# Inverting in halves of four matrices, and other shares of gathered rows for each layer, in a two-block transformer kernel

## Chip, cores and metric

The kernel runs on one core of one Trainium2 chip. The metric is the device time of one execution in microseconds. Three runs of the kernel before gave 3375.44 us in the median (3370.27 to 3380.55).

## The reference, cut to what matters

Two blocks work on 256 tokens of 1024 features in float32. The first block has two layers. In each, `h = rms_norm(x)`, one projection gives the inputs of three mixers (rwkv7, dilated attention, latent attention), their results go through `w_out`, and a gated feed-forward follows. The second block has two layers with attention and a PEER layer, for 256 latent tokens, and in its first layer also for 256 context tokens. The PEER layer picks 128 experts per token (8 heads, the best 16 each):

```python
u = u_tab[expert]                              # rows of 1024 numbers, one per slot
act = gelu(einsum('nhkd,nd->nhk', u, h))
out = einsum('nhk,nhkd->nd', g * act, v_tab[expert])
```

The rwkv7 scan is `state = state * w - (state kk) b + v k` over 256 steps. The kernel computes it in chunks of 64 steps, which needs the inverses of eight 128 x 128 unit triangular matrices (four heads, two tiles of 128 tokens; the two chunks of a tile lie on the matrix's diagonal).

## The kernel before, in words

**Stages.** The program is a row of stages. Each has its own code for each engine, and at its end TensorE (PE), ScalarE (ACT), VectorE (DVE) and SyncE (SP) join. First come the context tokens' own stages, then for each layer l = 0, 1 of the first block `in_projection`, `rwkv`, `latent_heads`, `first_attention`, `out_projection`, `feed_forward`, then the second block. GpSimd (POOL) doesn't join: it runs through one list of gathers on its own.

**Context rows.** The context tokens' PEER layer is independent of the first block, so its rows are spread over the first block's stages. There are 2 x 2 x 128 = 512 of them: for each half (blk) of the context tokens 128 rows of `u` (v = 0 in `order`) and 128 rows of `v` (v = 1). One row is a gather of 128 experts x 1024 float32, 0.524 MB, by `fetch` on POOL (L1318), and one instruction of 128x1024 on DVE: the dot product of a u row (L1338) or the weighted sum of a v row (L1335). `take(v, n, name)` (L1324 on) puts n of them into the code of a stage, `take_rest` the remainder of the stage's share. The shares are `SHARE` for either layer and `TAIL_SHARE` for the first attention of the second block. The u rows of half l must all lie ahead of layer l's feed-forward, where `weigh` makes the weights out of the dot products. `CTX_TAIL = 24` v rows of each half go to the end of the list.

**Places.** A row lands in one of four places of `ctx_ring`, or of four more in `ctx_more`. rwkv uses `ctx_more` for its matrices, so its rows have the four narrow places only (`wide` returns -1); in the other stages of the first block there are eight. POOL gathers a row into a place when DVE has used the place's last row (`ctx_used`).

**Weights.** SP loads groups of weights (2.1 MB for 4096 numbers per partition, in four pieces of 512 KB) into a ring of three slots. It loads group n + 3 when PE has finished group n.

**The inversion in rwkv (L579 to L771).** `b.inv` and `b.invT` hold eight matrices and their transposes. DVE masks the triangle (`keep(1, ...)`, L749), and for each of six levels selects the level's part into `b.ms` (L756). PE multiplies `ms` by `inv` (L586, 8 products, `w_done`), ACT copies the result to `b.ws` (L695), PE makes the updates of both (L597, L598, 16 products, `upd_done`), and DVE subtracts them from `inv` and `invT` in two instructions of 128x1024 (L770). Between these, PE does one half each of a group of modulation products (L1518, `mod_part`), and DVE takes six rows per level. Each float32 product is two passes in the trace. On DVE the order in a level is: wait for `w_done` of the level before, select, six rows, wait for `upd_done`, two subtractions. Everything works on all eight matrices at once.

**After it.** Four chunks with 2, 4, 4 and 4 rows, then the output (L793) with takes of 4, 2 and 3 rows as far as the share goes (4 and 1 here, L797 and L802 follow), and the group norm.

**Feed-forward.** PE computes 22 tiles of gate and up products (L1187), each of 32 products with a 128x256 result, into four buffers. Tile j waits for `acted` of tile j - 4. DVE multiplies gate and up (L1225, L1226) and then takes its rows: 2 or 3 by turns in layer 0, which also carries routing steps, 4 in layer 1. The down projection (L1199) follows, 352 passes, tile by tile in order of `acted`. DVE adds the result (L1244) when it is done.

## Time and profile before

| | us |
|---|---|
| median of 3 runs | 3375.44 |
| profiled execution, its time | 3365.98 |
| its span | 3364.1 |
| PE busy | 2677.2 (80%) |
| DVE busy | 2247.5 (67%) |
| POOL busy | 1211.3 (36%) |
| ACT busy | 586.3 (17%) |

The DMA engines moved 1029.23 MB, 306 GB/s in the mean. The chain that ended last is 39% PE, 30% DMA and 22% DVE. By place in the span: the context stages lie before 283 us, layer 0 of the first block from 283 to 926, layer 1 from 926 to 1548, and the second block behind that; its two PEER layers make the last 1500 us, with the DMA engines at 420 GB/s. Busy times are sums over stages with different limits, so they must be read stage by stage. Stage borders are read from the timelines.

### The profile page before, as it was taken

The numbers are of one execution on the slowest core, as the hardware profiler recorded it, in microseconds if no ns is written. First come the engines' busy times: TensorE is split into PE (matmuls) and PEld (weight loads), VectorE is DVE, ScalarE is ACT, GpSimd is POOL, SyncE is SP. The second block draws the span as 40 slices with busy tenths as digits, with TensorE's granted clock in tenths as the row PEclk, the third lists the DMA queues.
The fourth block names the chain that finished last, engine by engine and source line by source line (L and its number), as shares of the span: only waits on it lengthen the run. The fifth ranks groups of instructions, "written<-read, shape, count | busy, mean of one in ns | idle before, by whom it ended". The sixth has DMA issues, their size and how long they took to land.

```text
span 3364.1 us, 30927 instructions
## 1 busy us (share of the span) xinstructions
PE 2677.2 (80%) x10160; PEld 1779.6 (53%) x10160; DVE 2247.5 (67%) x5413; ACT 586.3 (17%) x1601; POOL 1211.3 (36%) x1028
## 2 busy tenths in 40 slices
PE   6898676899685869998887877777789977777776
PEld 2787555688574747886575332322247833323222
DVE  0538876788768576774958985655555499856555
ACT  1311201200011021001311111111124111111111
POOL 0002443345644424651323444444300044444442
PEclk8998776999897678998999999999989989999999
DMA  9337785789977657995657999999930379999997
GB/s 394 113 133 257 274 293 202 242 312 343 392 292 276 220 196 253 409 409 195 202 183 296 402 420 420 420 420 420 410 122 31 138 323 419 420 420 420 420 418 307
DMA packets 209376, 1029.23 MB, mean 306 GB/s; under 512 B 23392, under 2 KB 24928, under 8 KB 142784
## 3 DMA queue, kind: packets, MB, share of 16 engines
q0 software_dynamic: 147456, 805.37, 61.1%
q1 hardware_dynamic: 60480, 215.77, 17.1%
q10 hardware_dynamic: 1280, 6.11, 0.5%
q8 instruction: 81, 1.33, 0.2%
q14 instruction: 79, 0.65, 0.1%
HBM read 1021.98 MB, written 5.18 MB: 305 GB/s over the span
## 4 chain that ended last, share of the span: by engine, by line
PE 39%; DMA 30%; DVE 22%; issue 5%; ACT 2%; POOL 1%; SPq 1%; DVEq 0%; ACTq 0%; another core or an unknown queue 0%; POOLq 0%
DMA w_ring<-in_peer_uv,expert 16%; PE ps L1187 9%; PE ps L2251 4%; PE ps L1940 4%; DMA ctx_ring<-in_peer_uv,expert 4%; DMA own<-in_peer_uv,expert 4%; PE ps L1109 4%; PE ps L443 4%; PE ps L1648 3%; PE ps L1199 2%; DVE ctx_ring L1338 2%; DMA ctx_ring<-in_peer_u,ctx_expert 2%; DVE sum L1335 2%; DVE w_ring L2128 2%; DMA w_ring<-in_weights 2%
## 5 line engine op out<-in xcount | busy, mean ns | idle before, releaser
L2251 PE MATMUL ps<-w_ring,diag 128*128 128x512 f32 x1224 | 586.9, 620 | 177.4 <-ACT diag L2210 177.4
L2128 DVE SCALAR_TENSOR_TENSOR w_ring<-w_ring,htok 128x1024 f32<-128x1024 f32 x306 | 374.4, 1224 | 216.5 <-DMA w_ring<-in_peer_uv,expert 214.6
L2251 PEld LDWEIGHTS ps<-w_ring,diag 128*128 128x128 f32 x1224 | 228.7, 196 | 527.3 <-ACT diag L2210 286.6
L2098 POOL DMA_INDIRECT w_ring<-in_peer_uv,expert x306 | 337.5, 1103 | 447.7 <-PE ps L2251 396.7
L1318 POOL DMA_INDIRECT ctx_ring<-in_peer_u,ctx_expert x192 | 247.5, 1289 | 579.9 <-DVE ctx_ring L1338 299.1
L1187 PE MATMUL ps<-mix,w_ring 128*128 128x256 f32 x1408 | 309.3, 383 | 7.4 <-DVE mix L388 7.4
L1187 PEld LDWEIGHTS ps<-mix,w_ring 128*128 128x128 f32 x1408 | 270.8, 193 | 45.9 <-issue 8.2
L2210 ACT ACTIVATE diag<-consts_sb,w 128x128 f32<-128x128 f32 x512 | 177.6, 394 | 604.0 <-DVE w L2145 600.0
L1318 POOL DMA_INDIRECT ctx_ring<-in_peer_v,ctx_expert x148 | 184.0, 1243 | 235.4 <-DVE sum L1335 159.9
L2251 PE MATMUL ps<-ctx_ring,diag 128*128 128x512 f32 x416 | 212.0, 637 | 67.7 <-ACT diag L2210 67.7
L1338 DVE SCALAR_TENSOR_TENSOR ctx_ring<-ctx_ring,h_now 128x1024 f32<-128x1024 f32 x192 | 228.3, 1223 | 54.1 <-DMA ctx_ring<-in_peer_u,ctx_expert 46.2
L2098 POOL DMA_INDIRECT own<-in_peer_uv,expert x52 | 53.7, 1033 | 412.2 <-DVEq L1875 296.5
L1318 POOL DMA_INDIRECT ctx_more<-in_peer_v,ctx_expert x108 | 136.4, 1263 | 140.3 <-DVE low L1335 59.7
L2251 PEld LDWEIGHTS ps<-ctx_ring,diag 128*128 128x128 f32 x416 | 78.8, 199 | 190.1 <-ACT diag L2210 108.5
L2128 DVE SCALAR_TENSOR_TENSOR ctx_ring<-ctx_ring,htok 128x1024 f32<-128x1024 f32 x104 | 127.2, 1223 | 70.6 <-DMA ctx_ring<-in_peer_uv,expert 70.2
L2251 PE MATMUL ps<-own,diag 128*128 128x512 f32 x208 | 108.3, 645 | 81.3 <-ACT diag L2210 81.3
L2098 POOL DMA_INDIRECT ctx_ring<-in_peer_uv,expert x104 | 115.9, 1115 | 150.4 <-PE ps L2251 147.4
L1199 PE MATMUL ps<-act,w_ring 128*128 128x256 f32 x704 | 152.3, 379 | 0.0
L1199 PEld LDWEIGHTS ps<-act,w_ring 128*128 128x128 f32 x704 | 133.8, 190 | 18.2
L1940 PE MATMUL ps<-hT,w_ring 128*128 128x256 f32 x512 | 120.3, 391 | 13.3 <-DVE hT L385 13.3
L2205 ACT ACTIVATE th<-th 128x2 f32<-128x2 f32 x256 | 52.0, 203 | 450.2 <-DVE th L2137 450.2
L443 PE MATMUL ps<-mix,w_ring 128*128 128x256 f32 x544 | 119.7, 382 | 6.1 <-DVE mix L388 6.1
(402 smaller groups left out, 4553.9 us busy)
## 6 DMA issues: line engine op xcount, KB each, us to landing
w_ring<-in_weights SPq DMA_DIRECT2D x392, 512.0 KB, 8.0
w_ring<-in_peer_uv,expert POOLq DMA_INDIRECT x306, 15.9
ctx_ring<-in_peer_u,ctx_expert POOLq DMA_INDIRECT x192, 5.6
ctx_ring<-in_peer_v,ctx_expert POOLq DMA_INDIRECT x148, 8.8
consts_sb<-in_consts ACTq DMA_DIRECT2D x1, 1867.0 KB, 9.8
ctx_more<-in_peer_v,ctx_expert POOLq DMA_INDIRECT x108, 10.8
ctx_ring<-in_peer_uv,expert POOLq DMA_INDIRECT x104, 15.9
cT_first<-in_ctx_by_feature ACTq DMA_DIRECT2D x1, 1024.0 KB, 15.8
```

The source lines that it names most:

```text
L443: ins = pe.matmul(m.ps[:, j % BANKS, 0:SEQ], w[:, k, c:c + P], m.hT[:, k, 0:SEQ], start=(k == 0), stop=(k == KT - 1))
L1109: ins = pe.matmul(m.ps[:, j, 0:SEQ], w[:, k, (j % 4) * P:(j % 4 + 1) * P], src[:, k, 0:SEQ], start=(k == 0), stop=(k == KT - 1))
L1187: ins = pe.matmul(m.ps[:, GU[j % 4], part * SEQ:(part + 1) * SEQ], w[:, k, (j % 2) * P:(j % 2 + 1) * P], m.hT[:, k, 0:SEQ], start=(k == 0) ...
L1199: ins = pe.matmul(m.ps[:, 2 + o // 2, (o % 2) * SEQ:(o % 2 + 1) * SEQ], w[:, kk, o * P:(o + 1) * P], b.act[:, j, :], start=(j == 0 and o % ...
L1318: pool.indirect_dma_start(out=self.slot(r), out_offset=None, in_=expert_tables(self.d)[v], in_offset=bass.IndirectOffsetOnAxis(ap=m.ctx_ex ...
L1338: v.scalar_tensor_tensor(out=row, in0=row, scalar=1.0, in1=m.h_now[:, :], op0=ALU.mult, op1=ALU.mult, accum_out=m.ctx_dots[:, k:k + 1]).th ...
L1648: ins = pe.matmul(m.ps[:, j % 4, 0:width(j)], w[:, k, (j % 4) * P:(j % 4 + 1) * P], m.hT[:, k, 0:width(j)], start=(k == 0), stop=(k == KT ...
L1940: ins = pe.matmul(m.ps[:, j % 4, 0:SEQ], w[:, k, (j % 4) * P:(j % 4 + 1) * P], m.hT[:, k, 0:SEQ], start=(k == 0), stop=(k == KT - 1))
L2098: pool.indirect_dma_start(out=entry(e), out_offset=None, in_=table, in_offset=bass.IndirectOffsetOnAxis(ap=m.expert[:, blk, k:k + 1], axis ...
L2128: v.scalar_tensor_tensor(out=u, in0=u, scalar=1.0, in1=m.htok[:, blk, :], op0=ALU.mult, op1=ALU.mult, accum_out=b.dots[:, e:e + 1]).then_i ...
L2210: act.activation(b.diag[:, e % DIAGS, :], m.ident, ACT.Copy, scale=b.w[:, e:e + 1]).then_inc(s.built, 1)
L2251: ins = pe.matmul(m.ps[:, 2 * blk + half, :], b.diag[:, e % DIAGS, :], entry(e)[:, D + half * 512:D + (half + 1) * 512], start=(k == 0), s ...
```

## The change

It has two parts. (1) The inversion works in halves h of four matrices: PE, ACT and DVE signal each half on its own, the subtractions become four instructions of 128x512, `inv` and `invT` get a semaphore each, the next level is selected ahead of the subtractions, four rows are taken per level and none in level 0. (2) The shares are different for each layer; `CTX_TAILS` leaves 40 v rows of the first half and 24 of the second for later. Layer 1's feed-forward takes all 104 of its own half and the first 16 of the first half's 40.

| share | in_projection | rwkv | latent_heads | attention | out_projection | feed_forward |
|---|---|---|---|---|---|---|
| before, both layers | 28 | 64 | 8 | 16 | 12 | 104 |
| after, layer 0 | 36 | 56 | 8 | 16 | 12 | 88 |
| after, layer 1 | 36 | 56 | 8 | 16 | 12 | 120 |

The tail goes from 14, 18, 16 (project_qkv, attention, out_projection) to 16, 18, 14. `wide` is as before.

```diff
-CTX_TAIL = 24
+CTX_TAILS = (40, 24)
...
-                rows.take(v, 3, "in_projection")
+                rows.take(v, 4, "in_projection")
...
+        four = lambda i, h: m.ps[:, i + h, :].rearrange("p (c t) -> p c t", c=4)
...
                 pe.wait_ge(s.level_ready, lev + 1)
-                if lev:
-                    pe.wait_ge(s.upd_copied, 2 * lev)
-                for i in range(8):
-                    x = m.ident if lev == 0 else b.inv[:, i, :]
-                    ins = pe.matmul(m.ps[:, i // 4, (i % 4) * P:(i % 4 + 1) * P], b.ms[:, i, :], x,
-                                    start=True, stop=True)
-                ins.then_inc(s.w_done, 1)
+                for h in range(2):
+                    if lev:
+                        pe.wait_ge(s.inv_copied, 2 * (lev - 1) + h + 1)
+                    for i in range(4 * h, 4 * h + 4):
+                        x = m.ident if lev == 0 else b.inv[:, i, :]
+                        ins = pe.matmul(m.ps[:, h, (i % 4) * P:(i % 4 + 1) * P], b.ms[:, i, :], x, start=True, stop=True)
+                    ins.then_inc(s.w_done, 1)
...
                 mod_part(lev, 0, 1)
-                pe.wait_ge(s.w_copied, lev)
-                for i in range(8):
-                    xt = b.invT[:, i, :]
-                    pe.matmul(m.ps[:, 2 + i // 4, (i % 4) * P:(i % 4 + 1) * P], xt, b.ws[:, i, :], start=True, stop=True)
-                    ins = pe.matmul(m.ps[:, 4 + i // 4, (i % 4) * P:(i % 4 + 1) * P], b.ws[:, i, :], xt,
-                                    start=True, stop=True)
-                ins.then_inc(s.upd_done, 1)
+                for h in range(2):
+                    pe.wait_ge(s.w_copied, 2 * (lev - 1) + h + 1)
+                    pe.wait_ge(s.invT_copied, 2 * (lev - 1) + h + 1)
+                    for i in range(4 * h, 4 * h + 4):
+                        xt = b.invT[:, i, :]
+                        pe.matmul(m.ps[:, 2 + h, (i % 4) * P:(i % 4 + 1) * P], xt, b.ws[:, i, :], start=True, stop=True)
+                        ins = pe.matmul(m.ps[:, 4 + h, (i % 4) * P:(i % 4 + 1) * P], b.ws[:, i, :], xt, start=True, stop=True)
+                    ins.then_inc(s.upd_done, 1)
                 mod_part(lev, 1, 2)
...
-                act.wait_ge(s.w_done, lev + 1)
-                act.activation(b.ws[:, :, :], two_banks(0), ACT.Copy).then_inc(s.w_copied, 1)
+                for h in range(2):
+                    act.wait_ge(s.w_done, 2 * lev + h + 1)
+                    act.activation(b.ws[:, 4 * h:4 * h + 4, :], four(0, h), ACT.Copy).then_inc(s.w_copied, 1)
...
+            keep(1, b.mt, "before", 0)
+            select_level(0)
+            for h in range(2):
+                link(v.tensor_tensor(quad(b.invT, h), eye, quad(b.ms, h), ALU.subtract), s.invT_copied)
+            for h in range(2):
+                v.wait_ge(s.w_done, h + 1)
+                link(v.tensor_tensor(quad(b.inv, h), eye, four(0, h), ALU.subtract), s.inv_copied)
+            select_level(1)
+            keep(2, b.mkt, "before", 6)
+            for lev in range(1, LEVELS):
+                rows.take(v, 4, "rwkv")
+                if lev + 1 < LEVELS:
+                    v.wait_ge(s.w_done, 2 * lev + 2)
+                    select_level(lev + 1)
+                for dst, bk, copied in ((b.inv, 2, s.inv_copied), (b.invT, 4, s.invT_copied)):
+                    for h in range(2):
+                        v.wait_ge(s.upd_done, 2 * (lev - 1) + h + 1)
+                        link(v.tensor_tensor(quad(dst, h), quad(dst, h), four(bk, h), ALU.subtract), copied)
...
-                    rows.take(v, 4, "feed_forward")
+                    rows.take(v, 5, "feed_forward")
...
-        kept = SLOTS - CTX_TAIL
+        kept = [SLOTS - tail for tail in CTX_TAILS]
```

`select_level` is the selection of L756, and `quad(dst, h)` is half h of the eight matrices.

## Rows read from the trace of the kernel before

**Rows 1.** Windows: PE, PEld, DVE, ACT, POOL busy, PEclk, DMA share, GB/s.

```profile
283.00:363.50 80.50, 73.87 (x320) 63.64 (x320) 60.54 (x150) 13.20 (x32) 33.45 (x28) 0.94 0.78 281
399.60:480.50 80.90, 55.10 (x336) 41.27 (x336) 62.39 (x84) 8.11 (x10) 40.00 (x33) 0.77 0.81 284
894.00:926.00 32.00, 0.00 (x0) 0.00 (x0) 21.20 (x22) 0.04 (x1) 16.74 (x16) 0.54 1.03 409
1312.00:1469.60 157.60, 154.64 (x705) 135.78 (x706) 114.64 (x126) 11.21 (x25) 89.05 (x73) 0.98 0.96 378
1380.00:1410.00 30.00, 30.00 (x141) 26.41 (x140) 21.39 (x23) 1.82 (x5) 18.16 (x16) 1.00 1.03 409
```

**Rows 2.** DVE timeline, layer 0's inversion (start, us, line, [idle before]).

```profile
419.44 2.47 DVE L770 TENSOR_TENSOR ctx_more<-ctx_more,ps 128x1024 f32<-128x1024 f32 x2
...
435.65 2.47 DVE L770 TENSOR_TENSOR ctx_more<-ctx_more,ps 128x1024 f32<-128x1024 f32 x2
438.16 1.23 DVE L756 TENSOR_TENSOR ms<-ctx_more,consts_sb 128x1024 f32<-128x1024 f32 x1
439.42 1.23 DVE L1338 SCALAR_TENSOR_TENSOR ctx_ring<-ctx_ring,h_now 128x1024 f32<-128x1024 f32 x1
...
440.57 1.22 DVE L1338 SCALAR_TENSOR_TENSOR ctx_ring<-ctx_ring,h_now 128x1024 f32<-128x1024 f32 x1
...
477.95 2.47 DVE L770 TENSOR_TENSOR ctx_more<-ctx_more,ps 128x1024 f32<-128x1024 f32 x2
```

**Rows 3.** timeline of PE in the same inversion, level 2.

```profile
423.22 3.79 PE L586 MATMUL ps<-ctx_more,ms 128*128 128x128 f32 x16 [3.11 <-DVE ms L756]
426.94 1.94 PE L1518 MATMUL ps<-w_ring,silu 128*32 128x512 f32 x8
...
432.73 1.06 PE L1518 MATMUL ps<-w_ring,silu 128*32 128x512 f32 x8
```

**Rows 4.** chain of waits in the same inversion (start, us, what).

```profile
426.69 7.79 DMA ctx_ring<-in_peer_u,ctx_expert
...
471.59 5.19 DMA ctx_ring<-in_peer_u,ctx_expert
```

**Rows 5.** timeline of DVE, a 128x512 instruction that reads PSUM.

```profile
398.86 0.69 DVE L745 TENSOR_TENSOR rk<-ps,low 128x512 f32<-128x512 f32 x1
```

**Rows 6.** timeline of DVE at the end of layer 0's rwkv.

```profile
539.76 0.69 DVE L797 SCALAR_TENSOR_TENSOR yc<-ps,cum 128x512 f32<-128x512 f32 x1 [0.55 <-PE ps L653]
...
544.14 3.35 DVE L802 RECIPROCAL sq<-sq 128x512 f32<-128x512 f32 x1 [2.96 <-ACT sq L701]
```

**Rows 7.** timeline of DVE, end of layer 0's in_projection, start of rwkv.

```profile
354.07 1.23 DVE L1338 SCALAR_TENSOR_TENSOR ctx_more<-ctx_more,h_now 128x1024 f32<-128x1024 f32 x1 [1.54 <-DMA ctx_more<-in_peer_u,ctx_expert]
...
363.53 0.74 DVE L707 TENSOR_SCALAR kk<-low,vectors 128x256 f32<-128x256 f32 x2 [0.55 <-DVE ctx_weight L1893]
```

**Rows 8.** timeline of DVE at the end of layer 0's feed-forward.

```profile
883.21 1.28 DVE L1335 SCALAR_TENSOR_TENSOR sum<-ctx_ring,ctx_weight,sum 128x1024 f32<-128x1024 f32 x1 [1.22 <-DMA ctx_ring<-in_peer_v,ctx_expert]
...
923.23 2.48 DVE L1244 TENSOR_TENSOR xT<-xT,ps 128x512 f32<-128x512 f32 x4
```

**Rows 9.** timeline of PE in layer 0's feed-forward.

```profile
817.68 76.14 PE L1199 MATMUL ps<-act,w_ring 128*128 128x256 f32 x352
```

**Rows 10.** timeline of DVE, start of layer 1's rwkv.

```profile
1003.45 0.74 DVE L707 TENSOR_SCALAR kk<-low,vectors 128x256 f32<-128x256 f32 x2 [18.49 <-SPq L169]
```

**Rows 11.** timeline of DVE in layer 1's feed-forward.

```profile
1356.71 1.28 DVE L1335 SCALAR_TENSOR_TENSOR low<-ctx_more,ctx_weight,low 128x1024 f32<-128x1024 f32 x1 [0.56 <-DMA ctx_more<-in_peer_v,ctx_expert]
...
1489.60 0.41 DVE L1225 TENSOR_TENSOR act<-sg,ps 128x256 f32<-128x256 f32 x1
...
1545.66 2.48 DVE L1244 TENSOR_TENSOR xT<-xT,ps 128x512 f32<-128x512 f32 x4 [11.86 <-PE ps L1199]
```

**Rows 12.** timeline of DVE, end of the second block's first out_projection.

```profile
1720.62 0.48 DVE L1133 SCALAR_TENSOR_TENSOR xT<-ps,mods,xT 128x256 f32<-128x256 f32 x1
...
1727.86 1.75 DVE L379 RECIPROCAL htok<-htok 128x256 f32<-128x256 f32 x1 [0.34 <-DVEq L169]
```

More of the change, by code:

```diff
@@ L495, in rwkv @@
     sems = ("step_v step_a step_p acted lora_done ready_kk kk_sum kk_root ready_bonus bonus_sum bonus_used scaled turned tok_done "
-            "pairs_done masked level_ready w_done w_copied upd_done upd_copied rhs_done rhs_copied sa_done sa_copied "
+            "pairs_done masked level_ready w_done w_copied upd_done inv_copied invT_copied rhs_done rhs_copied sa_done sa_copied "
             "grow_done state_ready y_done y_copied mean_done centered var_done var_root act_tanh mod_done mod_copied mod_kept0 mod_kept1")
@@ L593, in _ @@
                 mod_part(lev, 0, 1)
-                pe.wait_ge(s.w_copied, lev)
-                for i in range(8):
-                    xt = b.invT[:, i, :]
-                    pe.matmul(m.ps[:, 2 + i // 4, (i % 4) * P:(i % 4 + 1) * P], xt, b.ws[:, i, :], start=True, stop=True)
-                    ins = pe.matmul(m.ps[:, 4 + i // 4, (i % 4) * P:(i % 4 + 1) * P], b.ws[:, i, :], xt,
-                                    start=True, stop=True)
-                ins.then_inc(s.upd_done, 1)
+                for h in range(2):
[6 more added lines that the diff above has]
+                    ins.then_inc(s.upd_done, 1)
                 mod_part(lev, 1, 2)
-            pe.wait_ge(s.upd_copied, 2 * LEVELS)
+            pe.wait_ge(s.inv_copied, 2 * LEVELS)
+            pe.wait_ge(s.invT_copied, 2 * LEVELS)
             pe.wait_ge(s.masked, 2)
@@ L750, in keep, with select_level @@
                                      ALU.mult), s.masked)
-            keep(1, b.mt, "before", 0)
-            for lev in range(LEVELS):
-                if lev:
-                    v.wait_ge(s.w_done, lev)
+            def select_level(lev):
                 link(v.tensor_tensor(b.ms[:, :, :], b.mt[:, :, :],
@@ L758, in _ @@
                      s.level_ready)
-                if lev == 0:
-                    keep(2, b.mkt, "before", 6)
-                rows.take(v, 6 if lev else 2, "rwkv")
-                if lev == 0:
-                    v.wait_ge(s.w_done, 1)
-                    eye = m.ident.unsqueeze(1).broadcast_to([P, 8, P])
-                    link(v.tensor_tensor(b.inv[:, :, :], eye, two_banks(0), ALU.subtract), s.upd_copied)
-                    link(v.tensor_tensor(b.invT[:, :, :], eye, b.ms[:, :, :], ALU.subtract), s.upd_copied)
-                    continue
-                v.wait_ge(s.upd_done, lev)
-                for dst, bk in ((b.inv, 2), (b.invT, 4)):
-                    link(v.tensor_tensor(dst[:, :, :], dst[:, :, :], two_banks(bk), ALU.subtract), s.upd_copied)
+            eye = m.ident.unsqueeze(1).broadcast_to([P, 4, P])
+            quad = lambda dst, h: dst[:, 4 * h:4 * h + 4, :]
+            keep(1, b.mt, "before", 0)
[16 more added lines that the diff above has]
+                        link(v.tensor_tensor(quad(dst, h), quad(dst, h), four(bk, h), ALU.subtract), copied)
             v.sem_inc(s.state_ready, 1)
@@ L1252 @@
 class ContextRows:
-    SHARE = dict(in_projection=28, rwkv=64, latent_heads=8, attention=16, out_projection=12, feed_forward=104)
-    TAIL_SHARE = dict(project_qkv=14, attention=18, out_projection=16)
+    FIRST_SHARE = dict(in_projection=36, rwkv=56, latent_heads=8, attention=16, out_projection=12, feed_forward=88)
+    SECOND_SHARE = dict(in_projection=36, rwkv=56, latent_heads=8, attention=16, out_projection=12, feed_forward=120)
+    TAIL_SHARE = dict(project_qkv=16, attention=18, out_projection=14)
     def __init__(self, m, d):
         self.m, self.d = m, d
-        kept = SLOTS - CTX_TAIL
-        self.order = [(blk, v, k) for blk in range(TT) for v, n in ((0, SLOTS), (1, kept)) for k in range(n)]
-        self.order += [(blk, 1, k) for blk in range(TT) for k in range(kept, SLOTS)]
+        kept = [SLOTS - tail for tail in CTX_TAILS]
+        self.order = [(blk, v, k) for blk in range(TT) for v, n in ((0, SLOTS), (1, kept[blk])) for k in range(n)]
+        self.order += [(blk, 1, k) for blk in range(TT) for k in range(kept[blk], SLOTS)]
         self.taken = 0
         self.ends, at, stage_of = {}, 0, []
-        for l, share in enumerate((self.SHARE, self.SHARE, self.TAIL_SHARE)):
+        for l, share in enumerate((self.FIRST_SHARE, self.SECOND_SHARE, self.TAIL_SHARE)):
             for name, n in share.items():
```

## The prediction

> **What bounds the kernel now.** I read the stages one by one in the windows, then the timelines of DVE and PE across each edit, the chain of waits inside the inversion, and at each stage's end the wait that was last. The second block's two PEER layers make the last 1500 us and aren't touched; all that counts lies between 283 and 1728 us.
>
> In the inversion DVE is on the path, and in it the rows. From one pair of subtractions to the next DVE needs (477.95 - 419.44) / 4 = 14.6 us [rows 2]. Of this 2.5 us are the two subtractions, 1.26 the selection (438.16 to 439.42), and the rest, over 10 us, six rows: four lie ready in the ring and cost 1.15 us each (439.42 to 440.57, rows 2), the last two wait for their gathers, which take 5.19 to 7.79 us from issue to landing [rows 4]. PE is done earlier. In level 2 it multiplies for 3.79 us, works 1.94 us on the modulation, about 3.9 us on the updates (to 432.73) and 1.06 us on the modulation again [rows 3], 10.5 us together, but DVE's subtraction comes 2.8 us after the updates, which ended at 432.7 (435.65, rows 2).
>
> Layer 0's in_projection ends with DVE's rows and the softmax of the routing at 363.5 [rows 7]. Its feed-forward ends with DVE too: PE's last product ends at 817.68 + 76.14 = 893.8 [rows 9], the addition starts at 923.23 [rows 8], and PE stands still between them, while the DMA engines are full at 409 GB/s [rows 1]. Layer 1's in_projection leaves DVE 18.5 us idle at its end [rows 10]. Layer 1's feed-forward ends with PE, DVE waits 11.86 us for it [rows 11]. So rows were too many in layer 0's feed-forward and there is room in layer 1, but how much room is the question of the sum.
>
> **Inversion (both layers).** Per level DVE has four rows (4 x 1.15 = 4.6), a selection (1.26) and four subtractions of 128x512. The nearest row, an instruction of that size on PSUM, takes 0.69 us and the next starts 0.72 later [rows 5]; with the wait on its own semaphore 0.73, so 2.92. Sum 8.8 us, if nothing stalls. PE's order lets it multiply the first half as soon as that half of `inv` is subtracted, while DVE does the other three, so its 10.5 us are the other bound; they hold both clock levels: 16 passes take 3.79 us after the 3.11 us wait, 0.23 each (1.2 GHz), while the updates' 32 passes take 3.9 us [rows 3], 0.12 each (2.4 GHz). With shorter waits the first part should run at the upper level more often (1.9 and 1.1 us), which gives 7.8. The ring is the third: a gather that starts 1.5 us after the first row and is landed 5.2 to 7.8 us later; the fourth is issued 6.0 us after the first row, so its place is ready at 11.2 to 13.8 and is wanted at 8.8 + 3.5 = 12.3. With the short landing nothing waits, with the long one 1.5 us. I take 9.6 us, halfway between 8.8 and 10.5: four intervals give 38.4 for 58.5, that is -20. The start (no rows in level 0, halves instead of the second wait for PE) lets the first subtraction begin at about 416 instead of 419.44 [rows 2], -3; the last four halves take 0.4 more than two wholes. Sum -23 per layer; bounds -26 (8.8) and -16 (10.5 everywhere and the start worth nothing).
>
> **End of rwkv.** The takes of 2 and 3 were cut to 1 and 0 by the share; now they are whole. Before L797 DVE waited 0.55 us after one row [rows 6]: a second row adds 0.6. Before L802 it waited 2.96 us: three rows take 3.45, and the third lies in a place freed only four microseconds earlier, so 1.5 more. Together +2.1 per layer (bounds 1 and 4). rwkv is thus -20.9 in each layer, -41.8 in both.
>
> **in_projection.** Eight more rows in each layer, 9.2 us of DVE. In layer 0 DVE is busy throughout, the last rows wait already (1.54 us, rows 7), and after them, from 356.6 to 362.4, it waits for ACT's softmax: 9.2 + 2 - 6 = +5 (bounds 3 and 9). In layer 1 they lie under the 18.5 us [rows 10]; but the stage now starts without the 32 us of full-rate transfers, and 0.5 to 4 us may come late: +1 (0 to 6).
>
> **Feed-forward of layer 0.** 16 fewer rows, all from its end, where they came one per 1.9 us (21 rows from 883.21 to 922.4, rows 8). DVE would be through at about 891, so PE's 893.8 ends the stage: 923.23 - 894.0 = -29.2. If the 13 last rows come later than now, DVE ends it: bound -25.
>
> **Feed-forward of layer 1.** This is where it is paid. The DMA engines are full there: 1380 to 1410 at 409 GB/s [rows 1]. A tile needs four rows (2.10 MB) and half a group of weights (1.05 MB). PE takes 7.03 us per tile (154.64 us for 22, rows 1) and so its weights take 149 GB/s, which leaves 260 for rows: one per 2.02 us. The trace agrees: from the first late row (the 19th, 1356.71) to tile 21's multiplication behind row 84 (1489.60) it is 132.9 us for 66 rows, 2.01 each [rows 11]. Five rows per tile then take 10.1 us, more than PE's 7.03, and PE may be only four tiles ahead. Tile j's products start at about 1315 + 7.03 j; the multiplication of tile j - 4 stands behind row 5 (j - 4), at 1277.4 + 10.1 j in this count. They meet at j = 12, and from 13 on PE waits. Both then share the DMA engines: (5 x 0.524 + 1.05) / 0.409 = 9.0 us per tile. Tile 21 starts at 1277.4 + 131.3 + 8 x 9.0 = 1480.7 instead of 1462.6: +18 at the down projection, which follows in 76.1 us, and so at the stage's end. The 11.86 us of DVE's slack don't help, since the delay arises ahead of the down projection. Bounds: +9, if only the end counts (16 rows at 1.28 us, full rate, less the slack), and +32, 16 rows at 2.02.
>
> The Trainium skill ("DMA: Bandwidth & Descriptors", section "Where 436 GB/s comes from") says that a transfer between HBM and SBUF is bound by the HBM side at about 358 GB/s per core. By that rule a tile would take 10.2 us and this term would be about +28. The trace disagrees, it holds 409 GB/s for 30 us at a time; the sum goes by the trace.
>
> **Tail.** project_qkv gets two rows more on a DVE that is the bound there, 2 x 1.25 = +2.5. out_projection gets two less: its last addition starts at 1720.62 and the next stage at 1727.86 [rows 12], where the same step without rows takes about 3 us. -4.2 (0 to -5).
>
> **Sum.** -41.8 + 5 + 1 - 29.2 + 18 + 2.5 - 4.2 = -48.7 us. The profiled execution, 3365.98 (span 3364.1), becomes 3317.3. It stands 9.5 below the median of the runs, so for the median 3375.4 - 48.7 = 3326.7, and 3327 is the forecast. The large uncertain terms are the level (2 x 5), layer 1's feed-forward (9 to 14) and the base (5). In quadrature that is about 17: 3312 to 3342 as the forecast's own range.
>
> **Rivals.**
> (a) *The rows in layer 1's feed-forward cost their full 2.02 us*, because PE's wait delays weights in turn: +32 instead of +18, 3341. For it: the DMA engines are at 1.03 there, nothing gives way. Against it: PE's wait itself lowers the weights' rate.
> (b) *They cost only what passes the end*: +9, and the inversion reaches 8.8: 3375.4 - 48.7 - 9 - 6 = 3312, with layer 0's in_projection at its lower bound 3310. For it: PE's buffers and the ring's prefetch, which I count coarsely. Against it: row 84's time, which fits the 2.02 to 1%.
> (c) *TensorE stays at 1.2 GHz in the whole inversion*, since its bursts get shorter and waits more frequent. 48 passes at 0.23 and 2 x 1.94 are 14.9 us per level, as long as now: the inversion gains nothing, 3375.4 - 48.7 + 46 = 3373, no change. For it: 3.79 us after each wait and a mean clock of 0.77 there [rows 1]. Against it: the updates are at full clock in each level already, and the waits shrink. The Trainium skill ("TensorE: Matmul & The Clock Gate", section "HAM oscillation — how this bites in real kernels") describes bursts of products between waits that start slow every single time; the first part of rows 3 agrees.
> (d) *Slower: the DMA engines bind the whole first block.* What leaves layer 0's feed-forward is 8.4 MB moved at 409 GB/s while PE stood still; if in_projection of layer 1 then waits for those bytes, 20.5 us are given back, the eight rows of each in_projection cost 8 x 2.02 = 16.2, layer 1's feed-forward +32, and the inversion stays at 10.5 (-16 + 2.1 per layer). Sum: 16.2 + 16.2 + 20.5 + 32 - 27.8 - 29.2 - 1.7 = +26, 3401. It decides if the share of in_projection, 0.78 in layer 0 [rows 1], comes to 1 with 4.2 MB more: 22.6 MB in 80.5 us become 26.8, 333 GB/s, below 409. That speaks against it.
> That the change doesn't do what it says isn't a case: the shares are read at build time and sum to 512, and `wide` is as before.
>
> **How the numbers follow.** Forecast 0.60, (a) 0.17, (b) 0.13, (c) 0.06, (d) 0.04. The range that holds 8 in 10 reaches to (b) with its spread below and past (a) above: 3303 to 3352. A measurement of this kernel tells 0.3%, 10 us, from none (its three runs span 0.3%). Faster by more than that: all of the forecast, (a) and (b), less a little, plus a part of (c): 0.90. Within it: 0.06. Slower: 0.04.
>
> **What would show it.** Inversion: starts of the selection (L756's successor) 9 to 10 us apart, and no row waiting over 1.5 us; at 14 or more (c) is right. PE's first part of a level at 1.9 us instead of 3.79. Layer 0's feed-forward: the addition within 1 us behind PE's last product, DVE waiting for PE. Layer 1: steps of 9 us per tile in the second half, tile products that wait for DVE's `act` (in sum about 18 us), a down projection without gaps, DVE done before it. Layer 0's in_projection: rwkv 3 to 9 us later from its start. The forecast is wrong if layer 1's in_projection ends with rows, if the down projection waits for weights, or if either inversion takes over 65 us between its first mask and the first chunk (81 now).

## The result, and the profile after

The kernel after takes 3333.15 us in the median of 4 runs (3328.32 to 3340.96), the kernel before in the same comparison 3376.32. The ratio is 0.9876, with a 95% interval of 0.9848 to 0.9903. The forecast was 3327. The profiled execution took 3328.75 (span 3326.9, before 3364.1), so the two traces differ by 37.2 us where the forecast's sum had 48.7. The differences by stage follow (two figures are layer 0 / layer 1; the marks are rounded, so the rows add to 37.5):

| stretch | before | after | difference | forecast |
|---|---|---|---|---|
| layer 0 in_projection | 80.4 | 86.0 | +5.6 | +5 |
| rwkv up to the first mask | 36.1 / 36.3 | 35.5 / 39.2 | +2.3 | 0 |
| first mask to last subtraction, layer 0 / 1 | 80.8 / 81.0 | 58.3 / 60.3 | -43.2 | -46 |
| chunks, to the copies of y | 55.7 / 63.1 | 63.2 / 57.1 | +1.5 | 0 |
| end of rwkv | 14.4 / 13.9 | 16.1 / 15.7 | +3.5 | +4.2 |
| latent heads to out_projection | 110.3 / 114.9 | 113.0 / 114.8 | +2.6 | 0 |
| layer 0 feed-forward | 262.4 | 233.0 | -29.4 | -29.2 |
| layer 1 in_projection | 77.4 | 77.3 | -0.1 | +1 |
| layer 1 feed-forward | 233.1 | 255.1 | +22.0 | +18 |
| second block's first attention stages | 182.2 | 180.0 | -2.2 | -1.7 |
| all else | | | -0.1 | 0 |

From its first mask to the first subtraction layer 0 now takes 420.18 - 406.34 = 13.8 us (19.9 before). The level in the inversion, DVE's timeline of layer 0, answers to [rows 2]. L780 is now four subtractions merged to one line, L757 the selection, L1349 a row:

```profile
420.18 2.85 DVE L780 TENSOR_TENSOR ctx_more<-ctx_more,ps 128x512 f32<-128x512 f32 x4
423.07 1.23 DVE L1349 SCALAR_TENSOR_TENSOR ctx_ring<-ctx_ring,h_now 128x1024 f32<-128x1024 f32 x1
...
428.78 1.23 DVE L1349 SCALAR_TENSOR_TENSOR ctx_ring<-ctx_ring,h_now 128x1024 f32<-128x1024 f32 x1 [3.33 <-DMA ctx_ring<-in_peer_u,ctx_expert]
...
431.33 1.23 DVE L1349 SCALAR_TENSOR_TENSOR ctx_ring<-ctx_ring,h_now 128x1024 f32<-128x1024 f32 x1 [1.32 <-DMA ctx_ring<-in_peer_u,ctx_expert]
...
432.48 1.22 DVE L757 TENSOR_TENSOR ms<-ctx_more,consts_sb 128x1024 f32<-128x1024 f32 x1
433.74 2.85 DVE L780 TENSOR_TENSOR ctx_more<-ctx_more,ps 128x512 f32<-128x512 f32 x4
...
441.87 1.23 DVE L1349 SCALAR_TENSOR_TENSOR ctx_ring<-ctx_ring,h_now 128x1024 f32<-128x1024 f32 x1 [1.65 <-DMA ctx_ring<-in_peer_u,ctx_expert]
...
444.28 2.85 DVE L780 TENSOR_TENSOR ctx_more<-ctx_more,ps 128x512 f32<-128x512 f32 x4
```

The four subtractions take 2.85 us. The steps are 13.6 and 10.5, then 9.0 and 8.5 (the next two starts are 453.29 and 461.83): the two long ones hold rows that wait for their gathers, 3.33 + 1.32 us in the first and 1.65 in the second. The same levels on PE, in answer to [rows 3] (L588 the products of `ms` and `inv`):

```profile
421.01 2.02 PE L588 MATMUL ps<-ctx_more,ms 128*128 128x128 f32 x16
422.96 1.06 PE L1529 MATMUL ps<-w_ring,silu 128*32 128x512 f32 x8
...
434.57 3.75 PE L588 MATMUL ps<-ctx_more,ms 128*128 128x128 f32 x16 [5.77 <-DVE ctx_more L780]
```

In this layer they ran at 1.2 GHz once (3.75 us), behind a wait of 5.77 us, and at 2.4 GHz in the other levels (2.02 to 2.05).

The ends of layer 0's in_projection (DVE; [rows 7]) and feed-forward (PE, then DVE; [rows 8, 9]):

```profile
362.24 1.23 DVE L1349 SCALAR_TENSOR_TENSOR ctx_more<-ctx_more,h_now 128x1024 f32<-128x1024 f32 x1 [4.28 <-DMA ctx_more<-in_peer_u,ctx_expert]
...
370.79 0.35 DVE L711 TENSOR_SCALAR kk<-low,vectors 128x256 f32<-128x256 f32 x1 [0.55 <-DVE ctx_weight L1904]
```

```profile
849.81 40.09 PE L1209 MATMUL ps<-act,w_ring 128*128 128x256 f32 x185
```

```profile
890.01 2.48 DVE L1254 TENSOR_TENSOR xT<-xT,ps 128x512 f32<-128x512 f32 x4 [1.38 <-PE ps L1209]
```

Layer 0's in_projection ends with rows, one of them 4.28 us late. Layer 1's ends with a row as well: PE is done at 967.3, the last row waits 1.32 us for its gather and starts at 968.57, and rwkv starts at 970.15. In rwkv three more rows wait, 3.2 us in all:

```profile
968.57 1.23 DVE L1349 SCALAR_TENSOR_TENSOR ctx_more<-ctx_more,h_now 128x1024 f32<-128x1024 f32 x1 [1.32 <-DMA ctx_more<-in_peer_u,ctx_expert]
...
973.70 1.23 DVE L1349 SCALAR_TENSOR_TENSOR ctx_ring<-ctx_ring,h_now 128x1024 f32<-128x1024 f32 x1 [0.54 <-DMA ctx_ring<-in_peer_u,ctx_expert]
...
976.28 1.23 DVE L1349 SCALAR_TENSOR_TENSOR ctx_ring<-ctx_ring,h_now 128x1024 f32<-128x1024 f32 x1 [1.34 <-DMA ctx_ring<-in_peer_u,ctx_expert]
...
978.84 1.23 DVE L1349 SCALAR_TENSOR_TENSOR ctx_ring<-ctx_ring,h_now 128x1024 f32<-128x1024 f32 x1 [1.33 <-DMA ctx_ring<-in_peer_u,ctx_expert]
```

The feed-forward of layer 0 ends with PE, and DVE waits for it. Layer 1's feed-forward on PE, where [rows 11] showed DVE waiting only at the end:

```profile
1259.81 85.63 PE L1197 MATMUL ps<-mix,w_ring 128*128 128x256 f32 x384 [3.71 <-DVE mix L388]
1347.47 7.14 PE L1197 MATMUL ps<-mix,w_ring 128*128 128x256 f32 x32 [2.02 <-DVE act L1236]
1356.49 8.86 PE L1197 MATMUL ps<-mix,w_ring 128*128 128x256 f32 x32 [1.88 <-DVE act L1236]
...
1419.68 16.84 PE L1197 MATMUL ps<-mix,w_ring 128*128 128x256 f32 x64 [3.23 <-DVE act L1236]
1436.36 76.14 PE L1209 MATMUL ps<-act,w_ring 128*128 128x256 f32 x352
```

384 records are 12 tiles; from the thirteenth on (j = 12) PE waits for `act`, and ten tiles take 1436.36 - 1347.47 = 88.9 us, 8.9 each in the mean (9.0 forecast, 7.03 without waits). Windows of the two kernels, first before (chunks of layer 0 and 1, feed-forward of layer 1), then after; the columns are those of [rows 1], so the third figure from the end is the granted clock, the mean of a stretch (0.5 is 1.2 GHz throughout, 1.0 is 2.4):

```profile
480.40:536.10 55.70, 46.99 (x304) 45.20 (x304) 29.69 (x55) 2.82 (x5) 24.81 (x18) 0.75 0.63 217
1120.70:1183.80 63.10, 54.35 (x304) 52.54 (x304) 29.70 (x56) 2.82 (x5) 24.80 (x18) 0.65 0.57 197
1312.50:1545.70 233.20, 230.67 (x1056) 202.36 (x1056) 156.67 (x164) 11.32 (x25) 121.51 (x100) 0.99 0.97 378
```

```profile
406.30:464.70 58.40, 42.98 (x336) 32.65 (x336) 49.81 (x73) 8.96 (x15) 26.04 (x21) 0.94 0.79 285
464.70:527.90 63.20, 54.46 (x304) 52.65 (x304) 29.71 (x55) 2.81 (x5) 24.75 (x18) 0.65 0.58 197
1069.70:1126.90 57.20, 48.42 (x304) 46.61 (x304) 29.72 (x56) 2.82 (x5) 24.75 (x18) 0.73 0.65 219
1257.40:1512.50 255.10, 239.10 (x1056) 205.96 (x1056) 176.62 (x179) 11.29 (x25) 145.23 (x116) 0.96 0.96 378
```

The inversion now runs at a mean clock of 0.94. The chunks, which the change doesn't touch, do the same 304 products in 55.7 to 63.2 us, and the clock goes with the length in both kernels: PE's idle time in a chunk phase (length less PE busy) is 8.7 to 8.8 us in all four. In the feed-forward PE is busy 8.4 us longer with the same products (a part of them at 1.2 GHz) and idle 13.5 us longer: 22.

### The profile page after: what moved, and what is told of

Same layout as the page of the kernel before. It is cut to its first block, busy times and chain, and to the rows that moved or that the text cites. A ratio compares the mean times of both kernels' runs of the same rounds, so it can differ in the third digit from the quotient of the medians.

```text
span 3326.9 us, 31010 instructions
## 1 busy us (share of the span) xinstructions
PE 2671.1 (80%) x10160; PEld 1773.6 (53%) x10160; DVE 2249.5 (68%) x5437; ACT 587.6 (18%) x1611; POOL 1216.9 (37%) x1028
## 3 DMA queue, kind: packets, MB, share of 16 engines
q0 software_dynamic: 147456, 805.37, 61.7%
## 4 chain that ended last, share of the span: by engine, by line
PE 35%; DMA 34%; DVE 21%; issue 5%; POOL 3%; ACT 1%; SPq 1%; DVEq 0%; ACTq 0%; POOLq 0%
DMA w_ring<-in_peer_uv,expert 16%; PE ps L1197 5%; PE ps L2262 5%; PE ps L1209 5%; PE ps L1951 4%; DMA own<-in_peer_uv,expert 4%; DMA ctx_ring<-in_peer_uv,expert 4%; PE ps L1119 4%; DMA ctx_ring<-in_peer_u,ctx_expert 3%; PE ps L1659 3%; DMA ctx_ring<-in_peer_v,ctx_expert 2%; DVE ctx_ring L1349 2%; DMA w_ring<-in_weights 2%; POOL ctx_ring L1329 2%; DVE w_ring L2139 1%
## 5 line engine op out<-in xcount | busy, mean ns | idle before, releaser
L2262 PE MATMUL ps<-w_ring,diag 128*128 128x512 f32 x1224 | 595.6, 629 | 171.7 <-ACT diag L2221 171.4
L1329 POOL DMA_INDIRECT ctx_ring<-in_peer_u,ctx_expert x184 | 237.1, 1288 | 558.8 <-DVE ctx_ring L1349 270.1
L1197 PE MATMUL ps<-mix,w_ring 128*128 128x256 f32 x1408 | 317.7, 389 | 21.0 <-DVE act L1236 13.6
L1349 DVE SCALAR_TENSOR_TENSOR ctx_ring<-ctx_ring,h_now 128x1024 f32<-128x1024 f32 x184 | 218.2, 1223 | 36.4 <-DMA ctx_ring<-in_peer_u,ctx_expert 28.5
L2262 PE MATMUL ps<-own,diag 128*128 128x512 f32 x208 | 107.1, 639 | 80.4 <-ACT diag L2221 80.4
L1329 POOL DMA_INDIRECT ctx_more<-in_peer_u,ctx_expert x72 | 89.2, 1240 | 113.8 <-DVE ctx_more L1349 52.2
## 6 DMA issues: line engine op xcount, KB each, us to landing
w_ring<-in_peer_uv,expert POOLq DMA_INDIRECT x306, 15.9
ctx_more<-in_peer_v,ctx_expert POOLq DMA_INDIRECT x108, 10.3
ctx_ring<-in_peer_uv,expert POOLq DMA_INDIRECT x104, 15.9
```

The costliest lines, as they stand in the source:

```text
L1197: ins = pe.matmul(m.ps[:, GU[j % 4], part * SEQ:(part + 1) * SEQ], w[:, k, (j % 2) * P:(j % 2 + 1) * P], m.hT[:, k, 0:SEQ], start=(k == 0) ...
L1329: pool.indirect_dma_start(out=self.slot(r), out_offset=None, in_=expert_tables(self.d)[v], in_offset=bass.IndirectOffsetOnAxis(ap=m.ctx_ex ...
L1349: v.scalar_tensor_tensor(out=row, in0=row, scalar=1.0, in1=m.h_now[:, :], op0=ALU.mult, op1=ALU.mult, accum_out=m.ctx_dots[:, k:k + 1]).th ...
L2262: ins = pe.matmul(m.ps[:, 2 * blk + half, :], b.diag[:, e % DIAGS, :], entry(e)[:, D + half * 512:D + (half + 1) * 512], start=(k == 0), s ...
```

## The experiments

Each is compared with runs of the kernel before on the same chip, whose median was between 3369 and 3377 us in the different comparisons. So kernels of different comparisons are told apart by their ratios and by the traces' stretches, not by a few microseconds between medians. All are edits of the kernel after, unless said. The tables give the same stretches as above, layer 0 / layer 1.

**1. Halves and rows apart.** First part (1) of the change without its fewer rows, called halves here: the split, the two semaphores, and the selection ahead of the subtractions.

```diff
-CTX_TAILS = (40, 24)                                  +CTX_TAILS = (24, 24)
-shares of the change                                  +28, 64, 8, 16, 12, 104 in both layers
-rows.take(v, 4, "rwkv")        # each level           +rows.take(v, 6, "rwkv")
```

> The inversion in halves, but the shares of before everywhere (28, 64, 104 in both layers, six rows in each level). My theory (the rows held the level, the halves only let PE overlap the subtractions): DVE still needs 6 x 1.15 + 1.26 + 2.9 = 11.1 us per level and two of its rows wait for their gathers, so 13 to 14 us per level instead of 14.6; first mask to last subtraction 76 to 80 us (before 80.8), about 3 to 5 us per layer, 3366 to 3372 in all. Rival (the halves alone make the gain): levels of 10.4 us as in the changed kernel, 60 us, 3336.

Shares only:

```diff
-for h in range(2): ...                     # PE, ACT, DVE by halves
+ins = pe.matmul(...) for all eight, one w_done, upd_done, upd_copied as before
+if lev: rows.take(v, 4, "rwkv")
```

> The new shares with the old inversion (all eight matrices at once), four rows per level and none in level 0. My theory: the level is now PE's chain, 2.5 of subtractions, 2 to 3.8 of the first products, 1.9 of the modulation and 3.9 of the updates, 10.5 to 12 us; inversion 62 to 68 us instead of 58.3 with the halves, so 3341 to 3352. Rival 1 (halves are worth nothing, only the rows counted): 58 us, 3333 as the changed kernel. Rival 2 (the halves were nearly all): 14 us per level, 78 us, 3372.

| | time, ratio (95%) | inversion | in_projection 0 | feed-forward |
|---|---|---|---|---|
| before | 3376.9 | 80.8 / 81.0 | 80.4 | 262.4 / 233.1 |
| halves only | 3372.1, 0.9987 (0.9973 to 1.0) | 81.6 / 79.9 | 77.9 | 262.6 / 233.1 |
| shares only | 3353.1, 0.9919 (0.9894 to 0.9945) | 69.4 / 71.2 | 87.6 | 233.2 / 255.9 |
| after | 3333.2, 0.9876 | 58.3 / 60.3 | 86.0 | 233.0 / 255.1 |

Halves alone are worth nothing that the runs can tell (I had expected inversions of 76 to 80 us), four rows alone 10 to 11 us per layer, both together 21 to 23. DVE's timeline with halves and six rows, then with four rows and no halves (L772 and L757 are its subtractions and selection):

```profile
434.81 2.85 DVE L780 TENSOR_TENSOR ctx_more<-ctx_more,ps 128x512 f32<-128x512 f32 x4
...
449.24 2.85 DVE L780 TENSOR_TENSOR ctx_more<-ctx_more,ps 128x512 f32<-128x512 f32 x4
```

```profile
438.63 2.48 DVE L772 TENSOR_TENSOR ctx_more<-ctx_more,ps 128x1024 f32<-128x1024 f32 x2 [5.07 <-PE ps L599]
441.14 1.23 DVE L757 TENSOR_TENSOR ms<-ctx_more,consts_sb 128x1024 f32<-128x1024 f32 x1
...
450.83 2.48 DVE L772 TENSOR_TENSOR ctx_more<-ctx_more,ps 128x1024 f32<-128x1024 f32 x2 [3.75 <-issue]
```

With six rows a step is 14.4 us and DVE's subtractions wait for no engine: PE's earlier finish is worth nothing. With four rows it is DVE that stands still for 3.75 to 5.07 us, and the step of 12.2 is PE's chain. Only where the rows no longer cover that chain do the halves shorten it, from 12.2 to 10.4 us. Which of their parts does it isn't shown. In the run without them PE also waits for the selection, which comes behind the subtractions there, and its first products are slower (3.42 us for 2.02):

```profile
442.42 3.42 PE L587 MATMUL ps<-ctx_more,ms 128*128 128x128 f32 x16 [2.83 <-DVE ms L757]
```

The selection's 1.26 us, taken out of the chain, could be most of the 1.8 us; no run has it ahead with whole matrices.

**2. Fewer rows per level.** First the rows within the chunks alone, then with two rows per level:

```diff
-rows.take(v, 4 if c else 2, "rwkv")        +rows.take(v, (4, 6, 5, 5)[c], "rwkv")
-rows.take(v, 4, "rwkv")  # ahead of y      +rows.take(v, 6, "rwkv")
```

> The changed kernel with nothing but the rows inside rwkv's recurrence moved: 4, 6, 5, 5 rows in the four chunks (2, 4, 4, 4 now) and 6 before the copies of y (4 now), so fewer at the stage's end. My theory: they lie in DVE's waits for PE (6.5, 5.4, 3.2 and 9.7 us of them), the chunks take as long as their clock wants (56 to 64 us), the end 14 instead of 16 us; 3329, no difference that can be measured. Rival (DVE's answers to PE come late behind the rows): 1.2 us for each of six rows per layer, +12, 3345.

```diff
-rows.take(v, 4, "rwkv")  # each level      +rows.take(v, 2, "rwkv")   (and the two lines above)
```

> As the kernel with the rows moved within the chunks, and two rows per level of the inversion instead of four (the other eight come later in rwkv). My theory (a level of 10.4 us is bound by DVE with its four rows and their gathers, PE's own chain is 8.3 to 9): levels of 8.5 us, first mask to last subtraction 50 to 52 us instead of 58.3; the later rows cost about 4, so 3321 to 3329. Rival (PE's chain is the bound at 10.4): 58 us as now, and the later rows +4 to +9 per layer, 3341 to 3350.

The first measured 3334.7 (0.9904, 0.9878 to 0.993), not to be told from the kernel after, with inversions of 58.3 / 58.9, chunks 63.4 / 63.5, end 14.4 / 14.8. The second measured 3313.6 (0.9842, 0.982 to 0.9864), with inversions of 48.4 / 48.1, chunks 60.0 / 61.7, end 15.9 / 16.0. The level with two rows:

```profile
433.60 0.69 DVE L780 TENSOR_TENSOR ctx_more<-ctx_more,ps 128x512 f32<-128x512 f32 x1 [0.27 <-PE ps L601]
435.39 2.13 DVE L780 TENSOR_TENSOR ctx_more<-ctx_more,ps 128x512 f32<-128x512 f32 x3 [1.10 <-PE ps L601]
...
441.34 0.69 DVE L780 TENSOR_TENSOR ctx_more<-ctx_more,ps 128x512 f32<-128x512 f32 x1 [0.27 <-PE ps L601]
```

A level takes 7.74 us, and now PE comes last, by 0.27 us ahead of the first subtraction and 1.10 ahead of the other three. So the level of 10.4 us was DVE's with its rows and their gathers. The moved rows cost the chunks nothing at the lowest clock only: with the old rows PE's idle time there is 8.6 to 8.8 us in all twelve chunk phases of six profiles, with the moved ones it is 8.8 us at a clock of 0.65, but 10.6 to 11.7 at 0.68 to 0.72.

**3. Layer 1's feed-forward.** Four rows per tile, the rest after the last tile; then 104 rows in both layers:

```diff
-rows.take(v, 5, "feed_forward")            +rows.take(v, 4, "feed_forward")
```

> The changed kernel with four rows behind each tile of layer 1's feed-forward instead of five; the other 32 of its 120 rows come after the last tile, beside the down projection. My theory (the fifth row delays the multiplications that PE waits for): the down projection starts 157 us after the stage's root as before (179 with five), PE ends at 233, and the stage ends there or up to 9 us later with the rows: 13 to 22 us below the changed kernel, 3311 to 3320. Rival (the rows' bytes cost their time wherever they stand, the DMA engines being full): 255 us again, 3333.

```diff
-feed_forward=88, 120; CTX_TAILS = (40, 24) +feed_forward=104, 104; CTX_TAILS = (24, 24); 4 per tile
```

> The changed kernel without the move of 16 rows from layer 0's feed-forward to layer 1's (104 and 104, four per tile). My theory: layer 0's feed-forward 29 us longer, its addition 262 us after its root, layer 1's 22 us shorter, 233 us: +7, 3340. Rival (what leaves the first comes back in the second by the same amount, as all of it are DMA bytes): 3333, no difference. Second rival (the 29 us are gone in either order because the start of layer 0's stage is earlier): 3311.

The first: 3327.8 (0.9859, 0.9834 to 0.9883), feed-forward of layer 1 249.4. The second: 3338.5 (0.9881, 0.9859 to 0.9903), feed-forwards 264.3 and 233.1, as with the shares of before. The move of 16 rows is thus worth 31 - 22 = 9 us by the traces; by the runs it is 5 us between the medians, with overlapping intervals. The first run missed my number: the down projection did start 156 us after the root, PE was done at 232, but DVE was not. Its last rows, and a window at the end of that stage:

```profile
1498.68 1.29 DVE L1346 SCALAR_TENSOR_TENSOR sum<-ctx_more,ctx_weight,sum 128x1024 f32<-128x1024 f32 x1 [1.27 <-DMA ctx_more<-in_peer_v,ctx_expert]
1501.24 1.28 DVE L1346 SCALAR_TENSOR_TENSOR sum<-ctx_more,ctx_weight,sum 128x1024 f32<-128x1024 f32 x1 [1.27 <-DMA ctx_more<-in_peer_v,ctx_expert]
```

```profile
## 3 DMA queue, kind: packets, MB, share of 16 engines
q0 software_dynamic: 866, 3.17, 53.0%
q1 hardware_dynamic: 823, 2.99, 50.0%
```

One row per 2.56 us: from 1490 to 1505 the gathers (q0) moved 3.17 MB and the weights (q1), fetched ahead for the next stage, 2.99. I had let the rows have the full rate there. The rows' bytes are 16 x 0.524 / 0.409 = 20.5 us, and 16.3 of them remain with the rows at the end of the stage (249.4 - 233.1); the fifth row per tile costs another 5.7. The Trainium skill ("DMA: Bandwidth & Descriptors", section "Queues, rings and completion order") says that each DMA engine goes round its queues packet by packet; the even split agrees.

**4. The 16 rows elsewhere.**

```diff
+early = [(0, 1, k) for k in range(kept[0], kept[0] + 16)]   # ahead of the second half's u rows
-in_projection=36, rwkv=56, ..., feed_forward=120   +in_projection=44, rwkv=64, ..., feed_forward=104
```

with the rows within the chunks of experiment 2 and four rows per tile in the feed-forward.

> 16 of the first half's last context rows (second table) are taken in layer 1's in_projection and rwkv (44 and 64 rows) and no longer in its feed-forward (104, four per tile); in rwkv's recurrence over the chunks DVE takes 4, 6, 5, 5 rows and 6 before the copies of y. My theory (layer 1's feed-forward is bound by its bytes, in_projection and the chunks aren't): its addition 233 us after the root instead of 255, in_projection of layer 1 at 77 to 80 us as before, rwkv of layer 1 at most 4 us longer: 15 to 20 us below the changed kernel, 3313 to 3318. Rival (the rows cost 1.2 to 2 us wherever they stand, since DVE or the engines are full there too): +16 to +20 in in_projection and rwkv, 3331 to 3335.

Measured 3327.6 (0.9878, 0.9858 to 0.9898). The feed-forward fell to 233.1, but in_projection of layer 1 rose from 77.3 to 96.2 us. Its last 18 us:

```profile
970.00:988.00 18.00, 0.00 (x0) 0.00 (x0) 9.88 (x17) 0.13 (x1) 4.68 (x5) 0.51 1.03 410
```

PE stands still, DVE does a row per 2.56 us again, the DMA engines are full at 410 GB/s. The rival of this run was right: the cost moved with the rows. Only eight of the 16 lie in this stage; they cost 18.9 us there and gave back 2.8 at the start of rwkv (36.4 us for 39.2), 2.0 us per row. The other eight, in rwkv, left PE idle for 13.0 us in the chunks of layer 1, for 8.8.

**5. The clock in the chunks.**

```diff
+fill = lambda n: n times pe.matmul(m.ps[:, 1, :], m.ident, vtok of 512 columns, start=True, stop=True)
+fill(3)     # ahead of the wait for the inversion's last subtractions
 ins.then_inc(s.grow_done, 1)
+if c + 1 < NCHUNK: fill(2)
```

> Products of 128x512 whose result nobody reads are added on TensorE where it waits: three behind the last update of the inversion and two behind each of the first three chunks' products. My theory (the clock fell from 2.4 to 1.2 GHz in the waits after the now shorter inversion, and that is what took back 7.5 us in layer 0): with the waits filled the granted clock in the chunks is over 0.9 and they take 46 to 52 us instead of 63 and 57; 3315 to 3322. Rival (the low clock comes from the thin products of the chunks themselves, 64 columns wide, not from the waits): clock 0.65 to 0.72 as now, the fillers take 1.3 us each and cost 0 to 8 us per layer, 3333 to 3345.

With only the first line, `fill(3)`:

> The changed kernel with only the three fillers behind the inversion's last update, none between the chunks. Theory A (the wait after the inversion is what loses the clock, afterwards it would stay): chunks of 49 to 52 us. Theory B (the waits between the chunks lose it too, as in layer 0 of the kernel before, where it fell in the second chunk): first chunk at 2.4 GHz, 9 us instead of 13, the later ones partly at 1.2, 54 to 59 us. I expect B, 3320 to 3330.

And both in the kernel before:

> The kernel before with the same fillers and nothing else. My theory (the chunks of the kernel before paid for the low clock too, 55.7 us in layer 0 and 63.1 in layer 1 at a granted clock of 0.75 and 0.65): 49 us in both, 21 us less, 3355; against the changed kernel with fillers (3303) the change is then worth more than the 43 us of the plain comparison, about 50. Rival (the low clock belongs to the halves only): 0 to -7 us, 3370.

| | time, ratio (95%), all runs | chunks | clock there |
|---|---|---|---|
| after | 3333.2, 0.9876, 3328 to 3341 | 63.2 / 57.1 | 0.65 / 0.73 |
| after, filled | 3303.4, 0.9805 (0.9785 to 0.9825), 3303 to 3308 | 49.1 / 48.7 | 0.93 / 0.96 |
| after, filled once | 3327.8, 0.9864 (0.9835 to 0.9894), 3319 to 3335 | 55.7 / 55.7 | 0.75 / 0.75 |
| before, filled | 3339.7, 0.9891 (0.9864 to 0.9918), 3338 to 3342 | 46.5 / 48.1 | 0.96 / 0.96 |

The same 16 products in the first chunk, in the kernel after and in the filled one:

```profile
468.82 3.73 PE L573 MATMUL ps<-r,kx 128*128 128x128 f32 x16
```

```profile
468.42 2.00 PE L573 MATMUL ps<-r,kx 128*128 128x128 f32 x16
```

Work whose result nobody reads shortens the two chunk phases by 22.5 us in the kernel after and 24.2 in the kernel before; the medians fall by 30 (24 by the ratios) and 36. One fill behind the inversion is not enough (theory B), although it cuts the wait ahead of the chunks from 2.97 to 0.71 us; the same 16 products come at 1.2 GHz again:

```profile
467.10 3.63 PE L573 MATMUL ps<-r,kx 128*128 128x128 f32 x16
```

Its chunks of 55.7 us are as long as the shortest unfilled ones. In the kernel before I had expected 21 us; the traces differ by 3364.1 - 3340.4 = 23.7, and the run profiled before was 10 us below its median. With the clock held in both, the change is worth 3340.4 - 3306.3 = 34.1 us by the traces (3339.7 - 3303.4 = 36.3 by the medians, 29 by the ratios), not the 50 that I had expected.

**6. All together, and the best.** Fillers, two rows per level, the rows within the chunks, four rows per tile:

```diff
 the edits of 2, 3 (first) and 5
```

> The fillers on TensorE, two rows per level with the rows within the chunks moved (4, 6, 5, 5, then 6), and four rows per tile in layer 1's feed-forward, together. If the three gains are of different places they add: chunks 49 us and inversion 48 us in both layers, feed-forward of layer 1 249 instead of 255, so 3333 - 23 - 20 - 6 = 3284; rows that now meet shorter waits in the chunks can cost 1 to 3 us per layer, 3284 to 3290. Rival (with the chunks at 49 us DVE's rows decide them, 20 rows and its own work being 40 us there): chunks of 55 us, 3296.

Measured 3308.8 (0.9798, 0.9771 to 0.9826), for the 3284 to 3290 that I had expected: inversions 48.1 / 50.3, but chunks of 61.3 in both layers at a clock of 0.86. DVE's fifth and later rows of a chunk wait there, and PE waits behind them:

```profile
470.54 1.22 DVE L1356 SCALAR_TENSOR_TENSOR ctx_ring<-ctx_ring,h_now 128x1024 f32<-128x1024 f32 x1 [1.89 <-DMA ctx_ring<-in_peer_u,ctx_expert]
...
473.21 1.22 DVE L1356 SCALAR_TENSOR_TENSOR ctx_ring<-ctx_ring,h_now 128x1024 f32<-128x1024 f32 x1 [1.44 <-DMA ctx_ring<-in_peer_u,ctx_expert]
```

```profile
474.90 0.79 PE L640 MATMUL ps<-k,ktok 128*128 128x128 f32 x2 [5.38 <-DVE ic L793]
```

The ring has four places, so a fifth row in a fast chunk is late. PE's idle time in the phase is 12.2 us, for 5.2 in the kernel that is only filled. So the last run keeps the change's rows and adds only the fillers and four rows per tile:

```diff
+fill(3), fill(2)                              # as in 5
-rows.take(v, 5, "feed_forward")               +rows.take(v, 4, "feed_forward")
```

> The changed kernel with the fillers between the chunks (as measured, 3303) and four rows per tile in layer 1's feed-forward (255 to 249.5 us in two runs); the rows of the inversion and the chunks as in the changed kernel, since twenty rows in the chunks cost what the clock gave. If the two gains add: 3303 - 5.5 = 3298, chunks 49 us, inversion 58.5. Rival (the weights fetched ahead during the longer end of the feed-forward are no gain later, and the clock varies): 3303, no difference.

Measured 3299.8 (3298.8 to 3301.7), 0.9778 (0.9763 to 0.9793): inversions 57.6 / 58.7, chunks 49.2 / 47.8, feed-forward 249.4. The best of all, 33 us below the kernel after.

## Why the prediction was right, and where it was off

*Inversion, -46 forecast, -43.2 measured.* The mechanism is shown: DVE's rows bound the level, PE's chain was behind them (experiments 1 and 2). The level came to 10.4 and 10.2 us in the two layers instead of 9.6. The three terms for DVE held (four rows, 1.26, and 2.85 for my 2.92); the waits for the ring were undersized, 4.65 us in one level and 1.65 in the next where I had allowed 1.5 at most. The levels that waited little, 9.0 and 8.5 us, are the 8.8 of the stall-free count. The trace of before could have warned me. I took four rows of a level as ready and two as late, but between 419.44 and 435.65 three were late, by 1.57, 3.25 and 0.49 us:

```profile
432.78 1.22 DVE L1338 SCALAR_TENSOR_TENSOR ctx_ring<-ctx_ring,h_now 128x1024 f32<-128x1024 f32 x1 [3.25 <-DMA ctx_ring<-in_peer_u,ctx_expert]
```

The start gained 6.0 us in layer 0 and 4.5 in layer 1, not 3. So in both layers together the levels gave 34.6 us for my 40 and the starts 10.5 for my 6: two misses of opposite sign, and it is in part luck that the term comes so close.

*Layer 0's in_projection and feed-forward, layer 1's in_projection.* +5.6, -29.4 and -0.1 for +5, -29.2 and +1. Over all profiles in_projection of layer 0 is 77.9 to 80.4 us with 28 rows (three profiles) and 86.0 to 89.0 with 36 (eleven), so +8.5 is the better figure, inside my bounds. In layer 1 one sign that was to prove the forecast wrong appeared: in_projection ends with a row, in this profile and in eight more of the ten with 36 rows there. Yet the stage takes 77.0 to 79.3 us in those ten and 77.1 to 77.5 in the three with 28, so the rows used up DVE's 18.5 us of idle time without going past it by more than 2 us. The sign was drawn too tight, and the term of +1 was right.

*Layer 1's feed-forward, +18 forecast, +22.0 measured.* PE waits from one tile before the one that I named (j = 12 for 13), in steps of 8.9 us for my 9.0; these ten tiles are 18.6 us. The rest is the first wait (2.0) and 1.3 from the twelve tiles ahead of it, 85.63 us for 12 x 7.03. The waits for `act` come to 13.6 us in sum, where I had said about 18: part of the delay is products at the lower clock. Rival (a), the full 2.02 us per row, would have been +32.

*What the forecast did not have.* Rows that wait at the start of layer 1's rwkv: +2.9 in this profile; up to the first mask it is 38.0 to 39.8 us in the ten profiles with 36 rows in in_projection, 35.5 to 36.3 in the three with 28. These are the late bytes that I had put at in_projection's end, where they are small. And the clock: in the latent stages of layer 0 +2.7, where it was 0.89 from 600 to 630 us (before, 1.00 from 607 to 637, at the same place), and in the chunks, +7.5 in layer 0 and -6.0 in layer 1. I took stages that the change doesn't touch as constant, but the twelve chunk phases of the six profiles in which nothing of them was changed lay between 55.7 and 64.9 us, at clocks from 0.75 to 0.63, with the same idle time of PE (8.6 to 8.8 us). Whether the halves make the low clock likelier stays open: whole matrices had 55.7, 63.1, 55.7 and 58.5 us, halves (after and experiments 1 and 3) 55.7 to 64.9 with a mean of 61.5; the spreads overlap.

*The base.* The profiled run before lay 10.3 us below the median of its comparison, the one after 4.4 below. That is why the medians differ by 43 us and the traces by 37. So the forecast for the median, 6 us off, came closer than its sum, 11.5 us off, and that is luck. The clock in the chunks is the likely cause: filled, the runs of a kernel span 3 to 5.5 us, those of the kernel before 10 to 18 and of the kernel after 12.6. It isn't shown, since the four runs of experiment 4 span 1.6 us unfilled.

*The other rivals.* (b) needed levels of 8.8 us; (c) a low clock in the inversion, which had 0.94; (d) would have lengthened in_projection: in layer 0 the DMA share is 0.85 at 324 GB/s (my count had 333), and in layer 1 it reaches 1.03 from 932 us on, but the stage didn't get longer. So 36 rows just fit; with 44 (d)'s mechanism appeared, at its price of 2.0 us per row (experiment 4).

## What to carry to other kernels

Where two engines take turns, find which covers which before splitting the work: halves were worth nothing under six rows and 11 us per layer under four. Where a gather shared full DMA engines with a prefetch, a row took 2.56 us, twice its bytes' time, and moving it to another full stage moved the cost along. Look at the granted clock of each stretch of thin, dependent products; a few wide products in their waits took 22 to 24 us off the chunks here, more than half of what the change itself gave.
